# A fused hybrid decoder trunk: gated linear attention on 64x64 tiles of the array, differential scores on row halves

## The chip, the cores and the metric

The kernel runs on one core of one Trainium2 chip. The metric is the device time of one execution in microseconds (us). The engines of a core are TensorE (PE in the profile, its weight loads PEld), VectorE (DVE), ScalarE (ACT), GpSimd (POOL) and SyncE (SP), which here issues the weight transfers.

## The reference, cut to what matters

Two layers, 256 positions (two blocks of 128), width 4096, all in float32. Each layer normalises x, multiplies by a large `w_in`, feeds four token mixers, gates their output and multiplies by `w_out`. Two of the mixers are touched.

```python
# GLA, per head, chunks of C=64 positions, dk=64, dv=128 (8 heads, 4 chunks)
q_dec = q * dk**-0.5 * exp(b);  k_dec = k * exp(-b);  k_state = k * exp(b_last - b)
A       = where(causal, q_dec @ k_dec.T, 0)          # intra-chunk, within 64 positions
U       = k_state.T @ v                              # state of one chunk, 64 x 128
state   = exp(b_last) * state + U                    # state at the start of the next chunk
o       = A @ v + q_dec @ state_at_start             # intra + inter
# differential attention, per head: two maps (c = 0, 1) of 64 dimensions each
s[c]    = q[:, c] @ k[:, c].T                        # block 0: 128 keys, block 1: 256 keys
```

The state at the start of the first chunk is zero.

## The kernel before, in words

**The main products.** A layer is 31 chunks `j` of 512 output columns (23 of `w_in`, 8 of `w_out`), and a chunk is 16 groups `g` of two 128-row slices of the weights. For each group SP brings 512 KB of weights into `w_raw` (L220), ScalarE rounds them to `w_hi` (`hi`, L376), VectorE makes the rest `w_lo` (`lo`, L705), and TensorE runs `chunk_group` (L1140): 12 matmuls of 512 columns, six for each block of 128 positions. The three weight buffers have four slots each, so ScalarE and VectorE are at most four groups ahead of TensorE. At the end of a chunk ScalarE copies the two `main` banks out (`project`), in its own program after `hi` of groups 0 and 1 of the next chunk.

**The mixers** are cut into pieces, and every engine's program has the same loop over layer, chunk and group: after its share of group `g` of chunk `j` an engine runs the pieces that are hooked there. An order written out by hand, so: a piece stands at a group number, and semaphores hold it until its inputs are there. On TensorE every piece goes between the last matmul of one group and the first of the next.

**GLA** handles two heads per unit, one unit in each of chunks 4 to 7 (four units per layer, eight in all). The two heads' 64 dimensions lie on partitions 0 to 63 and 64 to 127. TensorE's pieces (`gla`, L1213): g 1 logits (contraction over 33 rows, L1221), g 3 sums, g 6 four transposes and U, g 8 the intra scores AT, g 11 the outputs. U is three matmuls of 256 columns, one for each chunk of 64 positions but the last; the other half of the 128 contraction rows in `g_ks` is zero, and of the 128x256 result the two diagonal blocks are used. AT is four matmuls of 128 columns against `g_q0` or `g_q1`, in which the other head's rows are zero. The output is eight matmuls with 64 output partitions (inter, two column halves of the array) and four with 128 (intra):

```python
for bank, off, t, c in ((4, 0, 0, 0), (4, 256, 0, 1), (5, 0, 1, 0)):                    # U, L1245
    ins = mm(M[bank][:, off:off + 256], g_ks[:, t, c, :], Y[:, t, vcol:vcol + 2 * P], off == 0, True)
...
            mm(M[1][r, b * P:(b + 1) * P], (g_q0, g_q1)[h][:, t * P + c * DK:t * P + (c + 1) * DK],
               g_S[:, 2 * t + c, :], b == 0, False)                                     # inter, L1263
```

Between them VectorE makes the states from U (g 10, six instructions on 64 partitions, L742 to L750) and copies AT (g 11, L754), POOL masks it (`mask_intra`, L292), and ScalarE copies the transposes (g 10, L414 to L416). At g 15 ScalarE squares the outputs (L419), VectorE sums them (L757), ScalarE makes the reciprocal root (L389, L391) and VectorE scales (L763). In chunk 7 TensorE also turns the keys of the sliding-window mixer at g 10 (L1391), which ScalarE copies at g 13 (L429). In chunk 6 `turn_rx` (L1209) stands at g 11, right behind the GLA outputs.

**Differential attention** handles two heads in each of chunks 16 to 19 (16 units in all). "turn" at g 0 and g 7, "scores" at g 1 and g 8 (L1320 to L1325): for each of the two maps a matmul of 128 and one of 256 columns, contracting over 128 rows of which 64 are zero in `d_q[c]`.

A float32 matmul that is not of the rounded kind stands in the profile as two records. Sixteen records of an inter step are its eight matmuls.

## Time and profile before

| | us |
|---|---|
| median of 3 runs | 2926.52 (2926.36 to 2926.75) |
| the profiled execution's own time | 2925.76 |
| its span, first to last instruction | 2924.0 |
| TensorE matmuls busy | 2913.5 (100%) |
| TensorE weight loads busy | 2403.2 (82%) |
| VectorE busy | 1585.6 (54%) |
| ScalarE busy | 1460.5 (50%) |
| GpSimd busy | 59.1 (2%) |
| DMA engines, mean busy share | 0.61, 187 GB/s |

A matmul's record in the profile has a modelled end and reaches into the next one, so what a matmul costs is read from the distance between starts. Idle time of an engine that is not the bottleneck costs nothing.

### The profile page before, as it was taken

The numbers are of one execution on the slowest core, as the hardware profiler recorded it, in microseconds if no ns is written. First come the engines' busy times: TensorE is split into PE (matmuls) and PEld (weight loads), VectorE is DVE, ScalarE is ACT, GpSimd is POOL, SyncE is SP. The second block draws the span as 40 slices with busy tenths as digits, with TensorE's granted clock in tenths as the row PEclk, the third lists the DMA queues.
The fourth block names the chain that finished last, engine by engine and source line by source line (L and its number), as shares of the span: only waits on it lengthen the run. The fifth ranks groups of instructions, "written<-read, shape, count | busy, mean of one in ns | idle before, by whom it ended". The sixth has DMA issues, their size and how long they took to land.

```text
span 2924.0 us, 34611 instructions
## 1 busy us (share of the span) xinstructions
PE 2913.5 (100%) x13381; PEld 2403.2 (82%) x13381; DVE 1585.6 (54%) x2098; ACT 1460.5 (50%) x2077; POOL 59.1 (2%) x106
## 2 busy tenths in 40 slices
PE   9999999999999999999999999999999999999999
PEld 7878888888888888888888888888888888888887
DVE  6445555555666455444554445555556664554444
ACT  6344445555566555444554444455555665553333
POOL 2000000000000000000000000000000000000000
PEclk9999999999999999999999999999999999999999
DMA  8655556666555666666666555565656565666664
GB/s 255 194 164 168 159 171 183 186 184 181 175 166 166 194 187 194 216 221 201 217 200 182 177 160 160 174 185 180 185 170 185 159 179 177 202 202 204 226 221 165
DMA packets 282965, 546.47 MB, mean 187 GB/s; under 512 B 17753, under 2 KB 22497, under 8 KB 282801
## 3 DMA queue, kind: packets, MB, share of 16 engines
q1 hardware_dynamic: 272560, 524.88, 58.5%
q0 software_dynamic: 5552, 17.26, 2.0%
q10 hardware_dynamic: 4688, 2.13, 0.3%
q8 instruction: 105, 1.72, 0.2%
q14 instruction: 60, 0.48, 0.0%
HBM read 535.81 MB, written 8.39 MB: 186 GB/s over the span
## 4 chain that ended last, share of the span: by engine, by line
PE 99%; ACT 0%; issue 0%; DMA 0%; DVE 0%; SPq 0%; ACTq 0%
PE main L1138 93%; PE mixer L1138 5%; PE mixer L1353 0%; PE mixer L1178 0%; PE mixer L1166 0%; PE mixer L1289 0%; PE mixer L1329 0%; DMA w_raw<-in_w_in 0%; PE mixer L1209 0%; PE mixer L1316 0%; PE mixer L1317 0%; PE mixer L1279 0%; ACT w_hi L376 0%; DVE w_lo L705 0%; PE mixer L1239 0%
## 5 line engine op out<-in xcount | busy, mean ns | idle before, releaser
L1138 PE MATMUL main<-w_hi,act 128*128 128x512 f32 x7936 | 2523.9, 394 | 1.8 <-ACT stage L386 0.9
L705 DVE TENSOR_TENSOR w_lo<-w_raw,w_hi 128x1024 fp32r<-128x1024 f32 x992 | 1205.7, 1224 | 1161.6 <-ACT w_hi L376 1155.1
L1138 PEld LDWEIGHTS main<-w_hi,act 128*128 128x128 f32 x7936 | 1490.9, 188 | 318.7 <-ACT act_T L386 2.8
L1138 PE MATMUL main<-w_lo,act 128*128 128x512 f32 x3968 | 1546.0, 390 | 0.0
L376 ACT ACTIVATE w_hi<-w_raw 128x1024 fp32r<-128x1024 f32 x992 | 1042.2, 1058 | 1001.6 <-PE main L1138 935.0
L1138 PEld LDWEIGHTS main<-w_lo,act 128*128 128x128 f32 x3968 | 746.4, 188 | 149.1
L386 ACT ACTIVATE stage<-main,rstd 128x512 f32<-128x512 f32 x40 | 27.4, 684 | 59.0 <-PE main L1138 58.4
L386 ACT ACTIVATE act_T<-main,rstd 128x512 f32<-128x512 f32 x28 | 19.1, 682 | 71.4 <-PE main L1138 71.4
L386 ACT ACTIVATE mix_Y<-main,rstd 128x512 f32<-128x512 f32 x24 | 16.4, 682 | 68.2 <-PE main L1138 68.2
L685 DVE SCALAR_TENSOR_TENSOR act<-act_T,par,act 128x256 fp32r<-128x256 f32 x96 | 42.0, 479 | 15.2 <-ACT act L358 15.1
L937 DVE TENSOR_TENSOR mix<-mix,main 128x512 f32<-128x512 f32 x32 | 22.0, 688 | 42.6 <-PE main L1138 42.6
L358 ACT ACTIVATE act<-act_T,par 128x256 fp32r<-128x256 f32 x96 | 43.0, 495 | 0.1
L1138 PE MATMUL mixer<-act_T,mix 128*128 128x128 f32 (+1 forms) x256 | 39.6, 288 | 0.0
L1138 PEld LDWEIGHTS mixer<-act_T,mix 128*128 128x128 f32 x256 | 36.0, 191 | 4.1
L499 ACT ACTIVATE mix<-mixer 128x128 f32<-128x128 f32 x32 | 8.5, 273 | 58.6 <-PE mixer L1138 58.6
L389 ACT ACTIVATE small<-small,cst 128x2 f32<-128x2 f32 (+2 forms) x50 | 14.8, 295 | 29.9 <-DVE small L873 29.2
L315 POOL DMA_DIRECT2D out<-mix x15 | 11.0, 731 | 915.8 <-DVEq L939 915.8
L1138 PE MATMUL mixer<-mix 128*128 128x256 f32 (+2 forms) x160 | 29.2, 321 | 0.0
L1138 PEld LDWEIGHTS mixer<-mix 128*128 128x128 f32 (+1 forms) x160 | 22.8, 190 | 5.6 <-issue 2.8
L296 POOL TENSOR_SCALAR_AFFINE_SELECT act_T<-act_T 128x512 f32<-128x512 f32 x8 | 12.4, 1551 | 693.5 <-DVE act_T L754 693.5
L491 ACT ACTIVATE mix<-mix,small 128x128 f32<-128x128 f32 x32 | 12.6, 395 | 25.6 <-DVE small L896 25.6
L838 DVE SCALAR_TENSOR_TENSOR mix<-mix_Y,par,mix 128x255 f32<-128x255 f32 (+2 forms) x48 | 23.2, 484 | 1.7
(234 smaller groups left out, 1052.4 us busy)
## 6 DMA issues: line engine op xcount, KB each, us to landing
w_raw<-in_w_in SPq DMA_DIRECT2D x736, 512.0 KB, 3.7
w_raw<-in_w_out SPq DMA_DIRECT2D x256, 512.0 KB, 3.7
out<-mix POOLq DMA_DIRECT2D x15, 512.0 KB, 3.5
mix<-in_x POOLq DMA_DIRECT2D x8, 512.0 KB, 6.0
mix<-out POOLq DMA_DIRECT2D x8, 512.0 KB, 6.1
mix_Y<-in_x SPq DMA_DIRECT2D x7, 512.0 KB, 7.2
act_T<-in_lru_w_r ACTq DMA_DIRECT2D x16, 64.0 KB, 1.8
act_T<-in_lru_w_i ACTq DMA_DIRECT2D x16, 64.0 KB, 2.0
```

The source lines that it names most:

```text
L296: pool.affine_select(out=AT, in_=AT, compare_op=ALU.is_ge, fill=0.0, base=0, pattern=[[0, 4], [1, P]], channel_multiplier=-1).then_inc(G[" ...
L315: pool.dma_start(out[0, :, i * NC:(i + 1) * NC].rearrange("(t p) n -> p t n", p=P), x_new).then_inc(x_stored, 16)
L358: ins = act.activation(A[:, k, 0, :], F[:, k * SEQ:(k + 1) * SEQ], ACT.Copy, scale=par[:, layer, base + k:base + k + 1])
L376: act.activation(w_hi[:, n % HI, :, :], w_raw[:, n % RAW, :, :], ACT.Copy).then_inc(w_hi_ready, 1)
L386: act.activation(dst[:, t, :], main[t][:, :], func, scale=rstd[:, t:t + 1]).then_inc(main_free, 1)
L389: act.activation(dst, src, ACT.Ln, scale=1.0 / n, bias=eps[:, :]).then_inc(ln, 1)
L491: act.activation(d_p[:, b:b + P], d_s[:, b:b + P], ACT.Exp, bias=d_sm[:, 20 + c:21 + c], accum_out=d_sm[:, 24 + c:25 + c])
L685: ins = dve.scalar_tensor_tensor(out=A[:, k, 1, :], in0=F[:, k * SEQ:(k + 1) * SEQ], scalar=par[:, layer, base + k:base + k + 1], in1=A[:, ...
L705: dve.tensor_tensor(w_lo[:, n % LO, :, :], w_raw[:, n % RAW, :, :], w_hi[:, n % HI, :, :].bitcast(F32), ALU.subtract).then_inc(w_lo_ready, 1)
L838: dve.scalar_tensor_tensor(out=l_xc[:, 3 - q:SEQ], in0=rx[:, i, 0:SEQ - 3 + q], scalar=p(q), in1=l_xc[:, 3 - q:SEQ], op0=ALU.mult, op1=ALU ...
L937: dve.tensor_tensor(x_new[:, t, :], x_old[:, t, :], main[t][:, :], ALU.add).then_inc(main_free, 1)
L1138: return pe.matmul(out_, lhsT, rhs, start=start, stop=stop, skip_group_check=True)
```

## The change

**Places of the array.** U, AT and the inter products now contract over 64 rows and give 64 output partitions: each is on one of four 64x64 tiles of the array (row half by the operands' partitions, column half by the output's). U is six matmuls of 128 columns, now at g 9, AT eight of 64 columns behind it in the same piece, the inter product six of 128 columns at g 13 (the first chunk's zero state is left out), the intra product four on the whole array as before. The row halves write to different banks: U's by chunk (M[4], M[5]), AT's and the outputs' by head (M[0] and M[2]; M[1] and M[3]). The differential scores contract over 64 rows with 128 output partitions, one map on each row half. Zero filling of `g_ks`, `g_q0`, `g_q1` and `d_q` goes; `g_AT`'s off-diagonal blocks are zeroed once per layer.

**Hooks.** ScalarE's copy of the transposes goes from g 10 to g 8, VectorE's states from g 10 to g 11, TensorE's AT from g 8 to g 9 and its outputs from g 11 to g 13; `turn_rx` of chunk 6 from g 11 to g 14 with its copy in g 2 of chunk 7; the turn of the keys in chunk 7 from g 10 to g 14 with its copy at g 15.

```diff
...
-g_ks = F[:, 4096:4608].rearrange("p (t c n) -> p t c n", t=T, c=2)
-g_q0, g_q1, g_kT = F[:, 4608:4864], F[:, 4864:5120], F[:, 5120:5376]
+g_ks = F[:, 4096:4352].rearrange("p (t n) -> p t n", t=T)
+g_qT, g_kT = F[:, 4608:4864], F[:, 4864:5120]
...
-g_AT = F[:, 5888:6400]
+g_AT = F[:, 5888:6400].rearrange("p (t h n) -> p t h n", t=T, h=2)
...
-d_q = (cut(1024, 256), cut(1280, 256))
+d_qT = cut(1024, 256)
...
     def mask_intra(layer, i):
...
-        AT = g_AT.rearrange("p (u i) -> p u i", u=4)
...
-        pool.affine_select(out=AT, in_=AT, compare_op=ALU.is_ge, fill=0.0, base=0,
-                           pattern=[[0, 4], [1, P]], channel_multiplier=-1).then_inc(G["ATmasked"], 1)
-        pool.wait_ge(G["ATmasked"], u * 2 + 1)
-        pool.memset(AT[0:DK, :, DK:P], 0.0).then_inc(G["ATmasked"], 1)
+        for c in range(2):
+            r = slice(c * DK, (c + 1) * DK)
+            AT = g_AT[r, :, :, c * DK:(c + 1) * DK].rearrange("p t h n -> p (t h) n")
+            pool.affine_select(out=AT, in_=AT, compare_op=ALU.is_ge, fill=0.0, base=0,
+                               pattern=[[0, 4], [1, DK]], channel_multiplier=-1).then_inc(G["ATmasked"], 1)
...
-        if g == 10:
+        if g == 8:
...
-            act.activation(g_q0[0:DK, :], M[3][0:DK, 0:256], ACT.Copy)
-            act.activation(g_q1[DK:P, :], M[3][DK:P, 0:256], ACT.Copy)
-            act.activation(g_kT, M[3][:, 256:512], ACT.Copy).then_inc(G["qkT"], 1)
+            act.activation(F[:, 4608:5120], M[3][:, :], ACT.Copy).then_inc(G["qkT"], 1)
         if g == 15:
...
-            act.activation(g_sq, M[1][:, :], ACT.Square).then_inc(G["sq"], 1)
+            for h in range(2):
+                ins = act.activation(g_sq[:, h * 256:(h + 1) * 256], M[1 + 2 * h][:, 0:256], ACT.Square)
+            ins.then_inc(G["sq"], 1)
...
-        if g == 13:
+        if g == 15:
...
         if s == "turned":
...
-            act.wait_ge(diff_zero, layer + 1)
-            act.activation(d_q[0][0:DK, :], M[0][0:DK, 0:256], ACT.Copy, scale=par[0:DK, layer, Q_DQ:Q_DQ + 1])
-            act.activation(d_q[1][DK:P, :], M[0][DK:P, 0:256], ACT.Copy, scale=par[DK:P, layer, Q_DQ:Q_DQ + 1])
+            act.activation(d_qT, M[0][:, 0:256], ACT.Copy, scale=par[:, layer, Q_DQ:Q_DQ + 1])
...
-                if j == J_RX[0] + 1 and g == 13:
+                if j == J_RX[0] + 2 and g == 2:
                     copy_rx(layer, 0, 0, 4)
...
-            for c in range(2):
-                r = slice(c * DK, (c + 1) * DK)
-                ins = dve.tensor_tensor(g_ks[r, :, c, :], gk[r, :, i * P:(i + 1) * P],
-                                        v3(g_es)[r, :, :], ALU.mult)
-            ins.then_inc(G["kst"], 1)
-        if g == 10:
+            dve.tensor_tensor(g_ks, k, v3(g_es), ALU.mult).then_inc(G["kst"], 1)
+        if g == 11:
...
-            for c, (bank, off) in enumerate(((4, 0), (4, 256), (5, 0))):
-                if c:
-                    dve.wait_ge(G["S"], u * 3 + c)
-                for h in range(2):
-                    r = slice(h * DK, (h + 1) * DK)
-                    src = M[bank][r, off + h * P:off + (h + 1) * P]
-                    if c == 0:
-                        ins = dve.tensor_copy(g_S[r, 1, :], src)
-                    else:
-                        ins = dve.scalar_tensor_tensor(out=g_S[r, c + 1, :], in0=g_S[r, c, :],
-                                                       scalar=g_dec[r, c:c + 1], in1=src,
-                                                       op0=ALU.mult, op1=ALU.add)
+            for k, (bank, off) in enumerate(((4, 0), (5, 0), (4, P))):
+                src = M[bank][:, off:off + P]
+                if k == 0:
+                    ins = dve.tensor_copy(g_S[:, 1, :], src)
+                else:
+                    dve.wait_ge(G["S"], u * 3 + k)
+                    ins = dve.scalar_tensor_tensor(out=g_S[:, k + 1, :], in0=g_S[:, k, :],
+                                                   scalar=g_dec[:, k:k + 1], in1=src,
+                                                   op0=ALU.mult, op1=ALU.add)
                 ins.then_inc(G["S"], 1)
-        if g == 11:
             dve.wait_ge(G["AT"], u + 1)
-            dve.tensor_copy(g_AT, M[0][:, :]).then_inc(G["ATcopied"], 1)
+            for h in range(2):
+                for c in range(2):
+                    r = slice(c * DK, (c + 1) * DK)
+                    ins = dve.tensor_copy(g_AT[r, :, h, c * DK:(c + 1) * DK],
+                                          M[2 * h][r, 0:P].rearrange("p (t n) -> p t n", t=T))
+            ins.then_inc(G["ATcopied"], 1)
         if g == 15:
...
             for t in range(T):
                 for h in range(2):
-                    b = (2 * t + h)
-                    ins = dve.tensor_scalar(Y[:, t, vcol + h * P:vcol + (h + 1) * P], M[1][:, b * P:(b + 1) * P],
+                    b = 2 * h + t
+                    ins = dve.tensor_scalar(Y[:, t, vcol + h * P:vcol + (h + 1) * P],
+                                            M[1 + 2 * h][:, t * P:(t + 1) * P],
...
-                    dve.memset(g_ks, 0.0)
-                    dve.memset(g_q0, 0.0)
-                    dve.memset(g_q1, 0.0)
-                    dve.memset(g_S[:, 0, :], 0.0).then_inc(gla_zero, 1)
+                    dve.memset(F[:, 5888:6400], 0.0).then_inc(gla_zero, 1)
...
                     if g == 15:
-                        dve.memset(d_q[0], 0.0)
-                        dve.memset(d_q[1], 0.0).then_inc(diff_zero, 1)
...
             ins.then_inc(G["turned"], 1)
+        if g == 9:
             pe.wait_ge(G["kst"], u + 1)
...
                 pe.wait_ge(rx_F, layer * 4 + 2)
-            for bank, off, t, c in ((4, 0, 0, 0), (4, 256, 0, 1), (5, 0, 1, 0)):
-                ins = mm(M[bank][:, off:off + 256], g_ks[:, t, c, :], Y[:, t, vcol:vcol + 2 * P], off == 0, True)
+            for t, c in ((0, 0), (0, 1), (1, 0)):
+                r = slice(c * DK, (c + 1) * DK)
+                for h in range(2):
+                    ins = mm(M[4 + c][h * DK:(h + 1) * DK, t * P:(t + 1) * P], g_ks[r, t, h * DK:(h + 1) * DK],
+                             Y[r, t, vcol + h * P:vcol + (h + 1) * P], t == 0, True)
             ins.then_inc(G["U"], 1)
-        if g == 8:
             pe.wait_ge(G["qkT"], u + 1)
-            for t in range(T):
+            pe.wait_ge(G["dec"], u + 1)
+            for t in range(T):
+                for c in range(2):
+                    tok = slice(t * P + c * DK, t * P + (c + 1) * DK)
+                    for h in range(2):
+                        r = slice(h * DK, (h + 1) * DK)
+                        ins = mm(M[2 * h][c * DK:(c + 1) * DK, t * DK:(t + 1) * DK], g_kT[r, tok], g_qT[r, tok],
+                                 t == 0, True)
+            ins.then_inc(G["AT"], 1)
+        if g == 13:
+            pe.wait_ge(G["S"], u * 3 + 3)
+            for k in (2, 1, 3):
+                t, c = divmod(k, 2)
+                tok = slice(t * P + c * DK, t * P + (c + 1) * DK)
                 for h in range(2):
-                    b = 2 * t + h
-                    ins = mm(M[0][:, b * P:(b + 1) * P], g_kT[:, t * P:(t + 1) * P],
-                             (g_q0, g_q1)[h][:, t * P:(t + 1) * P], b == 0, True)
-            ins.then_inc(G["AT"], 1)
-        if g == 11:
-            pe.wait_ge(G["S"], u * 3 + 3)
-            for c in range(2):
-                r = slice(c * DK, (c + 1) * DK)
-                for t in range(T):
-                    for h in range(2):
-                        b = 2 * t + h
-                        mm(M[1][r, b * P:(b + 1) * P], (g_q0, g_q1)[h][:, t * P + c * DK:t * P + (c + 1) * DK],
-                           g_S[:, 2 * t + c, :], b == 0, False)
+                    r = slice(h * DK, (h + 1) * DK)
+                    mm(M[1 + 2 * h][c * DK:(c + 1) * DK, t * P:(t + 1) * P], g_qT[r, tok], g_S[r, k, :], k < 3, False)
             pe.wait_ge(G["ATmasked"], u * 2 + 2)
             for t in range(T):
                 for h in range(2):
-                    b = 2 * t + h
-                    ins = mm(M[1][:, b * P:(b + 1) * P], g_AT[:, b * P:(b + 1) * P],
+                    ins = mm(M[1 + 2 * h][:, t * P:(t + 1) * P], g_AT[:, t, h, :],
...
             pe.wait_ge(DF["qkT"], u + 1)
             for c in range(2):
-                mm(M[1 + c][:, 0:P], d_q[c][:, 0:P], d_kT[:, 0:P], True, True)
-                ins = mm(M[1 + c][:, P:3 * P], d_q[c][:, P:2 * P], d_kT, False, True)
+                r = slice(c * DK, (c + 1) * DK)
+                mm(M[1 + c][:, 0:P], d_qT[r, 0:P], d_kT[r, 0:P], True, True)
+            for c in range(2):
+                r = slice(c * DK, (c + 1) * DK)
+                ins = mm(M[1 + c][:, P:3 * P], d_qT[r, P:2 * P], d_kT[r, :], False, True)
             ins.then_inc(DF["scores"], 1)
...
-                if j == J_RX[0] + 1 and g == 11:
+                if j == J_RX[0] + 1 and g == 14:
                     turn_rx(layer, 0, 0, 4)
...
                     turn_rx(layer, 1, (4, 10).index(g), 4)
-                if j == J_KEYS and g == 10:
+                if j == J_KEYS and g == 14:
                     pe.wait_ge(K["kn"], layer + 1)
...
```

TensorE, U and AT of the first GLA unit. Before, U stands behind the transposes of g 6 (`mixer<-mix_Y,act_T`) and AT (`mixer<-act_T`) two groups later. The rows around U:

```order
L1138 MATMUL main<-w_hi,act 128x512
L1238 MATMUL mixer<-ident,mix 128x128
L1239 MATMUL mixer<-ident,mix 128x128
L1238 MATMUL mixer<-ident,mix 128x128
L1239 MATMUL mixer<-ident,mix 128x128
L1138 MATMUL mixer<-mix_Y,act_T 128x256 x3
L1138 MATMUL main<-w_hi,act 128x512
```

Of the change, at g 9:

```order
L1129 MATMUL main<-w_lo,act 128x512
L1129 MATMUL main<-w_hi,act 128x512
L1129 MATMUL mixer<-mix_Y,act_T 64x128 x6
L1129 MATMUL mixer<-act_T 64x64 x8
L1129 MATMUL main<-w_hi,act 128x512
L1129 MATMUL main<-w_lo,act 128x512
```

U has moved back three groups and stands ahead of AT, between the same two main matmuls.

TensorE, the scores of the first differential head, before:

```order
L1138 MATMUL main<-w_hi,act 128x512
L1138 MATMUL mixer<-mix 128x128
L1138 MATMUL mixer<-mix 128x256
L1138 MATMUL mixer<-mix 128x128
L1138 MATMUL mixer<-mix 128x256
L1138 MATMUL main<-w_hi,act 128x512
```

Of the change:

```order
L1129 MATMUL main<-w_lo,act 128x512
L1129 MATMUL main<-w_hi,act 128x512
L1129 MATMUL mixer<-mix 128x128 x2
L1129 MATMUL mixer<-mix 128x256 x2
L1129 MATMUL main<-w_hi,act 128x512
```

The two maps now take turns; the number of matmuls and their columns are the same.

ScalarE, the end of chunk 7 and the start of chunk 8, before (L429 is the copy of the turned keys, L419 to L391 the norm of the GLA outputs, L376 `hi`, L386 the copy of a main bank):

```order
L376 ACTIVATE w_hi<-w_raw 128x1024 x3
L429 ACTIVATE act_T<-mixer,par 128x512
L376 ACTIVATE w_hi<-w_raw 128x1024 x2
L419 ACTIVATE mix<-mixer 128x512
L389 ACTIVATE act_T<-act_T,cst 128x4
L391 ACTIVATE act_T<-act_T 128x4
L376 ACTIVATE w_hi<-w_raw 128x1024
L386 ACTIVATE stage<-main,rstd 128x512
```

Of the change:

```order
L376 ACTIVATE w_hi<-w_raw 128x1024 x7
L418 ACTIVATE mix<-mixer 128x256 x2
L389 ACTIVATE act_T<-act_T,cst 128x4
L391 ACTIVATE act_T<-act_T 128x4
L429 ACTIVATE act_T<-mixer,par 128x512
L376 ACTIVATE w_hi<-w_raw 128x1024
L386 ACTIVATE stage<-main,rstd 128x512
```

The copy of the keys now stands behind the norm, right ahead of `hi` of chunk 8's first group.

## Rows read from the trace of the kernel before

**Rows 1.** The profile's page: busy time by engine, and the chain that ended last
```profile
PE 2913.5 (100%) x13381; PEld 2403.2 (82%) x13381; DVE 1585.6 (54%) x2098; ACT 1460.5 (50%) x2077; POOL 59.1 (2%) x106
...
PE main L1138 93%; PE mixer L1138 5%; PE mixer L1353 0%; PE mixer L1178 0%; PE mixer L1166 0%; PE mixer L1289 0%; PE mixer L1329 0%; DMA w_raw<-in_w_in 0%; PE mixer L1209 0%; PE mixer L1316 0%; PE mixer L1317 0%; PE mixer L1279 0%; ACT w_hi L376 0%; DVE w_lo L705 0%; PE mixer L1239 0%
```

**Rows 2.** The page's costliest groups: count | busy us, mean ns | idle before, releaser
```profile
L1138 PE MATMUL main<-w_hi,act 128*128 128x512 f32 x7936 | 2523.9, 394 | 1.8 <-ACT stage L386 0.9
L705 DVE TENSOR_TENSOR w_lo<-w_raw,w_hi 128x1024 fp32r<-128x1024 f32 x992 | 1205.7, 1224 | 1161.6 <-ACT w_hi L376 1155.1
...
L1138 PE MATMUL main<-w_lo,act 128*128 128x512 f32 x3968 | 1546.0, 390 | 0.0
L376 ACT ACTIVATE w_hi<-w_raw 128x1024 fp32r<-128x1024 f32 x992 | 1042.2, 1058 | 1001.6 <-PE main L1138 935.0
...
L296 POOL TENSOR_SCALAR_AFFINE_SELECT act_T<-act_T 128x512 f32<-128x512 f32 x8 | 12.4, 1551 | 693.5 <-DVE act_T L754 693.5
```

**Rows 3.** Timeline, TensorE, GLA unit of chunk 5: start us, us, engine, line, what
```profile
221.35 1.46 PE L1138 MATMUL mixer<-mix_Y,act_T 128*128 128x256 f32 x6
...
222.89 0.40 PE L1138 MATMUL main<-w_lo,act 128*128 128x512 f32 x1
...
228.14 1.05 PE L1138 MATMUL mixer<-act_T 128*128 128x128 f32 x8
...
229.26 0.40 PE L1138 MATMUL main<-w_lo,act 128*128 128x512 f32 x1
...
236.98 0.39 PE L1138 MATMUL main<-w_hi,act 128*128 128x512 f32 x1
237.30 1.58 PE L1138 MATMUL mixer<-act_T 128*64 128x128 f32 x16
238.81 1.16 PE L1138 MATMUL mixer<-mix_Y,act_T 128*128 128x128 f32 x8
...
240.04 0.39 PE L1138 MATMUL main<-w_lo,act 128*128 128x512 f32 x1
```

**Rows 4.** Timeline, TensorE, differential scores of the first head in chunk 16
```profile
786.25 1.47 PE L1138 MATMUL mixer<-mix 128*128 128x128 f32 x8
...
787.79 0.39 PE L1138 MATMUL main<-w_lo,act 128*128 128x512 f32 x1
```

**Rows 5.** Timeline, TensorE, logits of chunk 4, contracting over 33 rows
```profile
204.84 0.39 PE L1138 MATMUL main<-w_hi,act 128*128 128x512 f32 x1
205.15 0.71 PE L1138 MATMUL mixer<-mix 33*128 33x128 f32 x4
...
206.13 0.39 PE L1138 MATMUL main<-w_lo,act 128*128 128x512 f32 x1
```

**Rows 6.** Two windows in the inter step, mixer matmuls: us, busy (records), granted clock, DMA
```profile
237.55:237.65 0.10, 0.10 (x3) 1.00 0.01 0
238.05:238.15 0.10, 0.10 (x7) 1.00 1.04 61
```

**Rows 7.** Timeline, weight loads of the inter step, [idle before]
```profile
237.30 1.34 PEld L1138 LDWEIGHTS mixer<-act_T 128*64 128x64 f32 x16 [0.35 <-issue]
```

**Rows 8.** Timeline, ScalarE and VectorE around the GLA norm and the state step, chunk 5
```profile
224.03 1.45 DVE L748 SCALAR_TENSOR_TENSOR act_T<-act_T,mixer 64x128 f32<-64x128 f32 x4
...
240.01 0.60 ACT L419 ACTIVATE mix<-mixer 128x512 f32<-128x512 f32 x1 [1.48 <-PE mixer L1138]
240.64 0.69 DVE L757 TENSOR_REDUCE act_T<-mix 128x4 f32<-128x512 f32 x1 [0.85 <-ACT mix L419]
241.36 0.30 ACT L389 ACTIVATE act_T<-act_T,cst 128x4 f32<-128x4 f32 x1 [0.75 <-DVE act_T L757]
241.69 0.20 ACT L391 ACTIVATE act_T<-act_T 128x4 f32<-128x4 f32 x1
```

**Rows 9.** Timeline, the turn of the keys in chunk 7 and ScalarE's copy of it
```profile
388.64 0.60 PE L1391 MATMUL mixer<-ident,mix 128*128 128x128 f32 x4
...
389.28 0.69 ACT L429 ACTIVATE act_T<-mixer,par 128x512 f32<-128x512 f32 x1 [2.04 <-PE mixer L1391]
```

More of the change, by code:

```diff
@@ L162, in hybrid_trunk @@
         gate_mult, gate_T, gate_F = sem("gate_mult"), sem("gate_turned"), sem("gate_ready")
-        gla_zero, diff_zero = sem("gla_zero"), sem("diff_zero")
+        gla_zero = sem("gla_zero")
         rx_out, rx_T, rx_F = sem("rx_out"), sem("rx_turned"), sem("rx_copied")
```

## The prediction

> **What bounds the kernel now.** I read the page first: TensorE is busy for the whole span, every other engine for about half of it, and the chain that ended last is 99% TensorE: 93% the main products, 5% the mixers' matmuls [rows 1]. Then the costliest groups: the main matmuls idle 1.8 us in all [rows 2], so no wait ends late anywhere. A microsecond of TensorE's queue is a microsecond of the kernel, and other engines count only where they would make TensorE wait. The granted clock is 1.00, TensorE's 2.4 GHz level [rows 6]; nothing in the change lets the engine idle, so it stays. Last, the timeline for the price of each piece. Between pieces a main matmul starts every 0.227 us: (236.98 - 229.26) / 34 [rows 3]. A piece costs the time from its first start to the second main start behind it, less one 0.227 (the first main record starts early and waits); with a change of array shape ahead of it I count from the last main start before, less two.
>
> **Prices before** [rows 3, 4]. U: 222.89 - 221.35 - 0.23 = 1.31. AT: 229.26 - 228.14 - 0.23 = 0.89, for eight records, so 0.112 for a record of 128 columns. Outputs: 240.04 - 236.98 - 0.45 = 2.61, of which the eight intra records take 0.90 and the inter step 1.71. Scores: 787.79 - 786.25 - 0.23 = 1.31 (eight records, two of 128 and two of 256 columns for each map).
>
> **Changing the shape of the array has a price.** The logits contract over 33 rows and so use a row part of the array: four records that would take 0.45 cost 206.13 - 204.84 - 0.45 = 0.84 [rows 5]. Going in and coming back costs 0.39. In the inter step the weights are 64 columns, not 128: their load is idle 0.35 us before the first [rows 7], and a first load of half the columns should take about half a record less, 0.05 (estimate), so I take 0.34 for a pair of changes into tiles with 64 columns. The inter products themselves then take 1.71 - 0.34 = 1.37.
>
> **Column tiles work side by side, and the engine looks ahead only a little.** Sixteen records in 1.37 us is 0.086 each, under 0.11. The windows show why: early in the step 3 records overlap a window of 0.1 us, later 7 do [rows 6]. The first eight records are on the left columns, the next eight on the right. Eight in a row take 8 x 0.11 = 0.88, so the right half ended 0.49 later: it started 0.49 after the left, when four and a half records of it had gone. I read this as a look-ahead of about three records past the running one, each tile with its own stream, its own weight load included. The change puts only two records in a row on a tile before it goes to the next, so this look-ahead is enough to keep all tiles fed.
>
> **The change part by part.** (Row halves are nowhere seen side by side before; I assume of them what the column halves show. Bounds in the rivals.)
>
> 1. *U and AT, one piece in 64x64 tiles at g 9.* U: six matmuls are 12 records of 128 columns; the order left, right on the upper rows, left, right on the lower, left, right on the upper gives the busiest tile four: 0.44. AT: 16 records of 64 columns, four for each tile, 0.055 each (half of 0.11, estimate): 0.22. With one hold-up of half a record by the look-ahead: 0.715. A pair of shape changes: 0.34. Sum 1.055 against 1.31 + 0.89 = 2.20: **-1.15** a unit. Bounds: with every record alone it would be 12 x 0.11 + 16 x 0.055 + 0.34 = 2.54, that is +0.34; below, nothing under 0.66 + 0.34.
> 2. *Inter product at g 13.* 12 records; the order is upper left, lower left, upper right, lower right, and the last two again. The right tiles have four records and start half a record late: 0.44 + 0.055 = 0.495 against 1.37: **-0.875**. The shape changes and the intra product are as before. One chunk's product less is in this (bound: 12 x 0.11 = 1.32, so -0.05 with every record alone).
> 3. *Scores.* Each map on its own row half, half of 1.31 each: 0.655; plus a pair of changes with 128 weight columns, 0.39: 1.045 against 1.31: **-0.27**. Alone: +0.39. This is the part in which a new price eats most of the gain.
>    The Trainium skill (TensorE: Matmul & The Clock Gate, Part 3) gives 3.07 times, not 4, for four row tiles of 512 columns; no run here shows row tiles yet. By that loss two row halves would take 1.31 / 1.53 = 0.86, the scores -0.06, and the sum would be some 3 us less of a gain.
> 4. *ScalarE's and VectorE's pieces.* Fewer and wider instructions; the mask on POOL shrinks from 1.55 us [rows 2] to two halves on a quarter of the elements each. All hidden as long as weights stay ahead, so what each moved wait holds up counts. At g 11 VectorE now waits for U and AT of g 9, with `lo` of group 12 behind it: three state steps and four small copies, at most the old 1.45 [rows 8] plus four of 0.3, and 1.22 for `lo` itself [rows 2] make 3.9 us after the piece; TensorE needs it after two groups, 5.4 us. Hidden, 1.5 us to spare. ScalarE's copy at g 8 waits for the transposes of g 6, with `hi` 9 and `lo` 9 behind: about 0.7 + 0.7 + 1.06 + 1.22 = 3.7 against 5.4. Hidden. The outputs move from g 11 to g 13 and the norm at g 15 is held longer; in chunks 4 to 6 `lo` of the next chunk is ready about 0.8 us early.
> 5. *The end of chunk 7.* There the copy of the keys stands behind the norm. Count from the last main start of g 13. The squares start 240.01 - 236.98 = 3.03 later before [rows 8], now 3.03 - 0.875 = 2.15; two squares of about 0.4, the sum 0.69, 0.30 and 0.20 with 0.03 between them end at 4.2. The turn of the keys starts after the outputs (1.73) and 13 main matmuls (2.95), at 4.7, and the copy 0.64 after that [rows 9], so it ends at 6.0. `hi` 1.06 and `lo` 1.22 [rows 2] follow: 8.2. TensorE comes to chunk 8 at 25 x 0.227 + 1.73 + 0.44 = 7.85. A new wait of **0.4 us**, once a layer: +0.8. It was hidden before because copy and norm were two groups and more earlier.
> 6. `turn_rx`, zero fills: nothing on TensorE beyond the same transposes in another place.
>
> Sum: 8 x (-1.15 - 0.875) = -16.2; 16 x (-0.27) = -4.3; +0.8. **-19.7 us**. The profiled execution's own time is 2925.76; it becomes 2906.1. The median shown is 0.76 above that execution, so I predict 2906.8.
>
> **The rivals.**
>
> *Issue sets the pace (chance 0.12).* The 0.49 of the inter step is also 8 x 0.061: if after the array has emptied TensorE issues one record in 0.061 us, whatever the tile, the rows look the same. Then U and AT take 28 x 0.061 + 0.34 = 2.05 (-0.15), the inter step 0.84 (-0.53), the scores 0.78 + 0.39 (-0.14): -5.5 - 2.3 + 0.8 = -7.0, 2919.5. Against it: the queue has many main matmuls of 0.227 in which to fill.
> The Trainium skill (same page, Part 1) gives 62 ns of the sequencer's firmware for a matmul when the hardware does not decode it, which is this pace; it would bind in AT above all.
>
> *Weight loads of the two row halves go one after the other (0.12).* A load takes as long as a record of 128 columns for 128 weight columns, half of that for 64. The scores then need eight loads in a row and the last record: 1.10 + 0.39 (+0.18); U and AT 0.94 + 0.34 (-0.93), inter 0.60 (-0.77): -13.6 + 2.9 + 0.8 = -9.9, 2916.6.
>
> *Row halves take turns altogether (0.07).* Column tiles still pair. U and AT 1.21 + 0.34 (-0.65), inter 0.93 (-0.44), scores 1.30 + 0.39 (+0.38): -8.7 + 6.1 + 0.8 = -1.8, 2924.7, within what can be told from no change.
>
> *The other side: each turn from one row half to the other empties the array (0.05).* A change of shape costs half a pair, 0.17 to 0.2, and if a change of row half does too, the 9 turns of U and AT, 5 of the inter step and 3 of the scores add 8 x 14 x 0.17 + 16 x 3 x 0.2 = 28.6 to the case before: +26.8, 2953. It makes the kernel slower as soon as a turn costs 1.8 / 160 = 0.011 us. For it: no row before shows a turn of row halves. Against it: the turn from left to right columns empties nothing [rows 6].
>
> The change does what it says: the order of the instructions shows the smaller matmuls. The last 0.02 is for waits on VectorE or ScalarE that I have not seen.
>
> **How the numbers follow.** The forecast has 0.62 and its own range is 2904 to 2910 (look-ahead a little longer or shorter, no wait or a double one in chunk 8, the skill's loss on row tiles). The range reaches up over the two rivals next to it, to 2921: 0.86 of the cases, of which some lie outside my sizes. Two tenths of a per cent are 5.9 us, about what a measurement of this kernel tells from no change. Faster by more: the forecast, the serial loads and most of the issue case, 0.82. Within: row halves in turns and the rest of the issue case, 0.12. Slower: 0.06.
>
> **What would show it.** In the profile after: U and AT as one piece that costs TensorE about 1.05 us between main matmuls, outputs about 1.73, scores about 1.05; many mixer records overlapping in one window of the 64x64 piece; one wait of some 0.4 us of a main matmul for `lo` at the start of chunk 8, none elsewhere; main matmuls still 0.227 apart. Wrong would be: records in the 64x64 piece 0.06 apart (issue), scores above 1.31 (row halves in turns or loads in a row), or main matmuls waiting for `lo` in every chunk end.

## The result and the profile after

| | before | after |
|---|---|---|
| median of the runs, us | 2926.44 (2925.84 to 2926.75, 4 runs) | 2905.09 (2904.76 to 2905.81, 4 runs) |
| the profiled execution's own time | 2925.76 | 2904.84 |
| span of the profiled execution | 2924.0 | 2903.1 |

The ratio is 0.9929, with a 95% interval of 0.9916 to 0.9941: 21.35 us between the medians, 20.92 between the two profiled executions. The forecast was 2906.8, in a range of 2903.5 to 2921.0. So the sum of -19.7 fell short by 1.2 us, or 6%; the other 0.5 us between forecast and median is that this median lies only 0.25 above its own profiled execution, where before's lay 0.76 in the three runs that the forecast had.

The page after, its line of busy times and the group of the main products, which answer to [rows 1, 2]:

```profile
PE 2892.3 (100%) x13461; PEld 2373.4 (82%) x13461; DVE 1576.7 (54%) x2080; ACT 1445.9 (50%) x2053; POOL 66.2 (2%) x106
...
L1129 PE MATMUL main<-w_hi,act 128*128 128x512 f32 x7936 | 2522.3, 394 | 2.0 <-ACT stage L386 0.9
```

TensorE is still busy from end to end, and the main products still wait for next to nothing. TensorE has 80 records more than before and is busy 21.2 us less (2892.3 against 2913.5): records are smaller and lie beside each other. The granted clock is 1.00 as before.

**U and AT.** The timeline of TensorE after, in the GLA unit of chunk 5 (start us, length us, engine, line, what), against the first four rows of [rows 3]:

```profile
229.44 0.39 PE L1129 MATMUL main<-w_hi,act 128*128 128x512 f32 x1
229.75 0.55 PE L1129 MATMUL mixer<-mix_Y,act_T 64*64 64x128 f32 x10
230.04 0.27 PE L1129 MATMUL mixer<-act_T 64*64 64x64 f32 x2
...
230.14 0.27 PE L1129 MATMUL mixer<-mix_Y,act_T 64*64 64x128 f32 x1
230.15 0.49 PE L1129 MATMUL mixer<-act_T 64*64 64x64 f32 x13
230.57 0.50 PE L1129 MATMUL main<-w_hi,act 128*128 128x512 f32 x1
230.90 0.39 PE L1129 MATMUL main<-w_lo,act 128*128 128x512 f32 x1
```

The piece costs 230.90 - 229.44 - 0.45 = 1.01 us, where U and AT were 1.31 and 0.89. Its 28 records (12 of U, 16 of AT) start between 229.75 and the first main record at 230.57: 0.82 / 28 = 0.029 us each. AT's first records (230.04) start while U's last are still to come (230.14): a tile that has done its part of U goes on alone.

**Outputs.** The same view, a little later, against the last four rows of [rows 3]:

```profile
241.35 0.39 PE L1129 MATMUL main<-w_hi,act 128*128 128x512 f32 x1
241.67 0.67 PE L1129 MATMUL mixer<-act_T 64*64 64x128 f32 x12
242.27 1.16 PE L1129 MATMUL mixer<-mix_Y,act_T 128*128 128x128 f32 x8
...
243.50 0.39 PE L1129 MATMUL main<-w_lo,act 128*128 128x512 f32 x1
```

243.50 - 241.35 - 0.45 = 1.70 us against 2.61. The intra records are what they were; the inter step went from 1.51 (237.30 to 238.81 [rows 3]) to 0.60 between the first starts.

**Scores.** The same view in chunk 16, against [rows 4]:

```profile
777.97 0.39 PE L1129 MATMUL main<-w_hi,act 128*128 128x512 f32 x1
778.29 0.93 PE L1129 MATMUL mixer<-mix 64*128 64x128 f32 x8
...
779.48 0.39 PE L1129 MATMUL main<-w_lo,act 128*128 128x512 f32 x1
```

779.48 - 777.97 - 0.45 = 1.06 us against 1.31.

**Overlap.** Two windows of 0.1 us, one in each kind of 64x64 piece, mixer matmuls alone (us, busy and how many records, granted clock, DMA), against [rows 6]:

```profile
229.85:229.95 0.10, 0.10 (x8) 1.00 1.11 430
241.85:241.95 0.10, 0.10 (x8) 1.00 0.22 82
```

Eight records reach into each window, where the column halves alone showed 3 and 7. A record's end is modelled, so the count tells how densely records start; the pace of 0.029 us a record above says the same.

**The new wait.** TensorE's waits in the whole span of after, without the two of its start (waited for: us in total, times, longest):

```profile
PE main L1129 <- ACT stage L386: 0.9, 2, 0.4
PE main L1129 <- DVE act L692: 0.6, 1, 0.6
PE main L1129 <- DVE w_lo L703: 0.5, 2, 0.2
```

The last line is new: two waits for `w_lo`, one a layer. The timeline shows the first, at the start of chunk 8:

```profile
396.89 0.39 PE L1129 MATMUL main<-w_hi,act 128*128 128x512 f32 x1
397.52 0.50 PE L1129 MATMUL main<-w_hi,act 128*128 128x512 f32 x1 [0.24 <-DVE w_lo L703]
397.86 0.40 PE L1129 MATMUL main<-w_lo,act 128*128 128x512 f32 x1
398.10 0.62 PE L1129 MATMUL main<-w_hi,act 128*128 128x512 f32 x2
398.56 0.39 PE L1129 MATMUL main<-w_lo,act 128*128 128x512 f32 x1
```

The second start is 0.63 behind the first instead of 0.227, so 0.40 late; with the stretched step behind it (0.34) the loss is 397.86 - 396.89 - 0.45 = 0.52. In return another loss is gone. This is the same place in the trace of before:

```profile
406.47 0.91 PE L1138 MATMUL main<-w_hi,act 128*128 128x512 f32 x2
407.21 0.39 PE L1138 MATMUL main<-w_lo,act 128*128 128x512 f32 x1
```

There the second bank began late: 407.21 - 406.47 - 0.45 = 0.29, against 398.56 - 398.10 - 0.45 = 0.01 after. Net 0.52 + 0.01 - 0.29 = +0.24 a layer. The second of these losses stands in no wait of TensorE's matmuls. The weight loads' own list (PEld) has it: before, in chunk 8, the load for the second bank waits 0.44 us for ScalarE's copy (L386).

The account, from the starts on record, which have one digit more than the view prints: U and AT 1.30 + 0.90 to 1.02, the outputs 2.60 to 1.69, so 8 x (-1.18 - 0.91) = -16.7; each scores piece 0.27 less, so 16 x (-0.27) = -4.3; chunk 8 in both layers 2 x 0.24 = +0.5. That makes -20.5 of the measured -20.92. Of the other 0.4, 0.23 is a stop ahead of chunk 28 of the second layer that the trace of before has and that of after has not (2790.24 - 2789.56 - 0.45); no cause of it is on record. The start of the kernel varies by more than that: in the profiled executions of all these kernels the first twelve main matmuls took from 4.3 to 5.7 us (before 4.9, after 5.1).

### The profile page after: what moved, and what is told of

It reads as the page before. It is cut to its first block, busy times and chain, and to the rows that moved or that the text cites. A ratio compares the mean times of both kernels' runs of the same rounds, so it can differ in the third digit from the quotient of the medians.

```text
span 2903.1 us, 34721 instructions
## 1 busy us (share of the span) xinstructions
PE 2892.3 (100%) x13461; PEld 2373.4 (82%) x13461; DVE 1576.7 (54%) x2080; ACT 1445.9 (50%) x2053; POOL 66.2 (2%) x106
## 4 chain that ended last, share of the span: by engine, by line
PE 99%; ACT 0%; issue 0%; DVE 0%; DMA 0%; SPq 0%; ACTq 0%
PE main L1129 93%; PE mixer L1129 4%; PE mixer L1351 0%; PE mixer L1169 0%; PE mixer L1157 0%; PE mixer L1284 0%; PE mixer L1327 0%; DMA w_raw<-in_w_in 0%; PE mixer L1312 0%; PE mixer L1200 0%; PE mixer L1274 0%; PE mixer L1311 0%; ACT w_hi L376 0%; DVE w_lo L703 0%; PE mixer L1230 0%
## 5 line engine op out<-in xcount | busy, mean ns | idle before, releaser
L376 ACT ACTIVATE w_hi<-w_raw 128x1024 fp32r<-128x1024 f32 x992 | 1041.4, 1058 | 966.8 <-PE main L1129 909.4
L386 ACT ACTIVATE act_T<-main,rstd 128x512 f32<-128x512 f32 x28 | 19.1, 682 | 68.2 <-PE main L1129 68.2
L386 ACT ACTIVATE stage<-main,rstd 128x512 f32<-128x512 f32 x40 | 27.3, 684 | 38.3 <-PE main L1129 37.7
L386 ACT ACTIVATE mix_Y<-main,rstd 128x512 f32<-128x512 f32 x24 | 16.4, 682 | 59.2 <-PE main L1129 59.2
L298 POOL TENSOR_SCALAR_AFFINE_SELECT act_T<-act_T 64x256 f32<-64x256 f32 x16 | 21.9, 1370 | 681.3 <-DVE act_T L747 680.8
```

The lines of the kernel that those rows point to most:

```text
L298: pool.affine_select(out=AT, in_=AT, compare_op=ALU.is_ge, fill=0.0, base=0, pattern=[[0, 4], [1, DK]], channel_multiplier=-1).then_inc(G[ ...
L376: act.activation(w_hi[:, n % HI, :, :], w_raw[:, n % RAW, :, :], ACT.Copy).then_inc(w_hi_ready, 1)
L386: act.activation(dst[:, t, :], main[t][:, :], func, scale=rstd[:, t:t + 1]).then_inc(main_free, 1)
```

## The experiments

Theory T, from the prediction: tiles stream and load side by side, row halves as well as column halves; each tile keeps about three records behind the running one; a change of the array's shape has a price of its own. Rivals: issue at 0.06 us a record sets the pace; row halves do not pair, or load in a row. Later a fourth, on what the look-ahead is. Where no span is named, times are medians, with the kernel before run on the same chip. The 95% intervals are 5 to 10 us wide, so the small steps rest on the timelines.

### The two halves of the change, alone

Scores on row halves in the kernel before, with one copy of the queries instead of two zero-filled ones:

```diff
...
                     for c in range(2):
-                        mm(M[1 + c][:, 0:P], d_q[c][:, 0:P], d_kT[:, 0:P], True, True)
-                        ins = mm(M[1 + c][:, P:3 * P], d_q[c][:, P:2 * P], d_kT, False, True)
+                        r = slice(c * DK, (c + 1) * DK)
+                        mm(M[1 + c][:, 0:P], d_qT[r, 0:P], d_kT[r, 0:P], True, True)
+                    for c in range(2):
+                        r = slice(c * DK, (c + 1) * DK)
+                        ins = mm(M[1 + c][:, P:3 * P], d_qT[r, P:2 * P], d_kT[r, :], False, True)
```

> The kernel before with the differential scores alone on row halves; GLA as before. If row halves stream and load side by side: each of the 16 scores pieces falls from 1.31 to about 1.04 us between main matmuls (0.655 of stream, 0.39 for a pair of shape changes), 16 x 0.27 = 4.3 us less, about 2922. If the two row halves took turns: 16 x 0.38 = 6 us more, about 2932. If only their weight loads did: 16 x 0.18 = 3 us more.

The kernel after with this part taken back:

```diff
...
                     for c in range(2):
-                        r = slice(c * DK, (c + 1) * DK)
-                        mm(M[1 + c][:, 0:P], d_qT[r, 0:P], d_kT[r, 0:P], True, True)
-                    for c in range(2):
-                        r = slice(c * DK, (c + 1) * DK)
-                        ins = mm(M[1 + c][:, P:3 * P], d_qT[r, P:2 * P], d_kT[r, :], False, True)
+                        mm(M[1 + c][:, 0:P], d_q[c][:, 0:P], d_kT[:, 0:P], True, True)
+                        ins = mm(M[1 + c][:, P:3 * P], d_q[c][:, P:2 * P], d_kT, False, True)
```

> The changed kernel with the scores back on the whole array against zero-filled queries (and the zero fill back), GLA on 64x64 tiles as changed. If the terms are additive: 4.3 us more than the changed kernel, about 2909.4, and 17 us less than the kernel before: 8 x (1.15 + 0.9) less 1. If GLA's gain leant on the scores' (a shared wait on VectorE or ScalarE), it would be off by a microsecond or more.

The scores alone: 2921.19 (2920.76 to 2922.35, 10 runs) against 2926.26, ratio 0.9983 (0.9974 to 0.9993), -5.1 us. The GLA part alone: 2910.31 (2908.83 to 2910.75), ratio 0.9944 (0.9929 to 0.9959), 5.2 us above the whole change, and its GLA pieces stay at 1.02 and 1.70. In the first one's timeline the scores of chunk 16 have their last main start before at 785.96 and the second behind at 787.47: 1.51 - 0.45 = 1.06, with no GLA change near them. -0.27 x 16 = -4.3 explains most of the -5.1; the two parts add (5.07 + 15.95 = 21.0 of 21.35). Loads in a row (1.49) and row halves in turns (1.69) are out.

### AT apart from U

AT waits one group longer, so that the engine changes its shape twice instead of once.

```diff
                     ins.then_inc(G["U"], 1)
+                if g == 10:
                     pe.wait_ge(G["qkT"], u + 1)
```

> The changed kernel with AT one group later than U (g 10, not g 9), so two pieces in 64x64 tiles in place of one. If the price is the change of shape: one more pair of changes a unit, 8 x 0.34 = 2.7 us more, 2907.8, perhaps 0.05 more a unit since AT no longer fills U's idle tiles (3.1). If changing the shape cost nothing and the 0.39 of the logits came from the 33 rows: no difference.

Measured 2908.89 (2908.16 to 2909.69), ratio 0.994 (0.9925 to 0.9955); that is 3.8 above after; the span is 2906.4, 3.3 above after's. TensorE's timeline, U and then AT of chunk 5:

```profile
229.41 0.39 PE L1129 MATMUL main<-w_hi,act 128*128 128x512 f32 x1
229.73 0.65 PE L1129 MATMUL mixer<-mix_Y,act_T 64*64 64x128 f32 x12
...
230.65 0.40 PE L1129 MATMUL main<-w_lo,act 128*128 128x512 f32 x1
...
232.94 0.39 PE L1129 MATMUL main<-w_hi,act 128*128 128x512 f32 x1
233.26 0.46 PE L1129 MATMUL mixer<-act_T 64*64 64x64 f32 x16
...
233.99 0.39 PE L1129 MATMUL main<-w_lo,act 128*128 128x512 f32 x1
```

0.79 and 0.60 make 1.39 against 1.01: a second pair of changes costs 0.38 us, in which lies whatever is lost because AT no longer starts beside U's last records. 8 x 0.38 = 3.0 of the 3.3. The sixteen records of AT end within 0.60 with that pair in it; one each 0.06 us would need 1.0 for issue alone.

### What the look-ahead is

First the inter step of after, by heads: three matmuls on tiles of the upper rows, then three on the lower.

```diff
...
-                    for k in (2, 1, 3):
-                        t, c = divmod(k, 2)
-                        tok = slice(t * P + c * DK, t * P + (c + 1) * DK)
-                        for h in range(2):
+                    for h in range(2):
+                        for k in (2, 1, 3):
+                            t, c = divmod(k, 2)
+                            tok = slice(t * P + c * DK, t * P + (c + 1) * DK)
...
```

> The changed kernel with the six inter products ordered by head: upper left, upper right twice, lower left, lower right twice, instead of turning between heads. Same matmuls, same tiles. If the engine looks only some three records past the running one: the lower tiles start later, the step grows from 0.49 to about 0.65 us, 8 x 0.16 = 1.3 us more (2906.4). If it looked over the whole queue, or if issue at a fixed pace set the time: within 0.1 us a unit of the changed kernel.

Measured 2905.32 (2905.01 to 2905.81), ratio 0.9928 (0.9911 to 0.9944): no difference from after. The outputs stand between main starts at 241.62 and 243.78: 2.16 - 0.45 = 1.71, against 1.70. This was a miss of mine: I had expected the lower tiles to start late, as if the engine saw a fixed stretch of its queue. They don't, so that stretch is not what limits. What fits this and the 0.49 of before is that a record is held up only when its own tile, or the tile of one ahead of it in the queue, has about three waiting: here no tile gets more than four in a row. That reading says what the kernel before would do if its eight left records came in runs of four:

```diff
...
-                    for c in range(2):
-                        r = slice(c * DK, (c + 1) * DK)
-                        for t in range(T):
+                    for t in range(T):
+                        for c in range(2):
+                            r = slice(c * DK, (c + 1) * DK)
...
```

> The kernel before with its eight inter products in another order: four records on the left columns, four on the right, and again, in place of eight and eight. Only the order changes. If each tile can hold about three records behind the running one, whatever stands on other tiles: both halves start together, the inter step falls from 1.37 to 0.88 us of stream, 8 x 0.49 = 3.9 us less, 2922.5. If the engine looks over a fixed stretch of the whole queue (six loads and matmuls not yet issued): the right half starts a record late each time, stream about 1.2, 1.3 us less. If issue at 0.061 us a record set the 0.49: stream 0.98 + 0.05, 2.7 us less.

Measured 2922.52 (2921.93 to 2923.1, 10 runs) against 2926.14, ratio 0.9988 (0.9978 to 0.9997). Its inter step on TensorE:

```profile
236.92 0.39 PE L1138 MATMUL main<-w_hi,act 128*128 128x512 f32 x1
237.24 1.15 PE L1138 MATMUL mixer<-act_T 128*64 128x128 f32 x16
238.32 1.16 PE L1138 MATMUL mixer<-mix_Y,act_T 128*128 128x128 f32 x8
...
239.55 0.39 PE L1138 MATMUL main<-w_lo,act 128*128 128x512 f32 x1
```

From the first inter start to the first intra start it is 1.08 us instead of 1.51 [rows 3], with the same sixteen records in another order: -0.43 x 8 = -3.4, and -3.6 was measured between the medians. The expectation had -0.49 for it, a fixed stretch of the queue -0.16 and issue at a fixed pace -0.34. So 0.43 of the 0.91 us that the change gains on the outputs could be had without 64x64 tiles, by order alone. (The change also leaves out the first chunk's product. No run has that part alone. By the prices it saves nothing: that product lies on the left columns, and the busiest tile has four records with it or without.)

Last, the scores of after with each map's two matmuls together, runs of four for each row half:

```diff
                         mm(M[1 + c][:, 0:P], d_qT[r, 0:P], d_kT[r, 0:P], True, True)
-                    for c in range(2):
-                        r = slice(c * DK, (c + 1) * DK)
                         ins = mm(M[1 + c][:, P:3 * P], d_qT[r, P:2 * P], d_kT[r, :], False, True)
```

> The changed kernel with each map's 128-column and 256-column scores behind each other (the order of before, four records in a row on a row half) instead of the maps taking turns. With about three records held behind the running one for each tile: no difference (piece 1.06 us). With a look-ahead over a fixed stretch of the whole queue: the second map starts a record late, 0.11 us a piece, 16 x 0.11 = 1.8 us more.

Measured 2904.78 (2904.6 to 2904.89), ratio 0.9926 (0.9911 to 0.9941): no difference from after, as a run of four should. The profiled execution even started 0.5 us faster than after's. The interleaving of the scores in the change is not needed.

### The wait at chunk 8

The turn of the keys and its copy two groups and one group earlier:

```diff
-                if g == 15:
+                if g == 14:
                     act.wait_ge(K["turned"], layer + 1)
...
-                        if j == J_KEYS and g == 14:
+                        if j == J_KEYS and g == 12:
                             pe.wait_ge(K["kn"], layer + 1)
+                            pe.wait_ge(G["ATcopied"], layer * 4 + 4)
```

> The changed kernel with the turn of the keys at g 12 (not 14) and ScalarE's copy at g 14 (not 15), ahead of the norm. If the 0.54 us that the keys' piece costs above its four transposes is ScalarE's late hi of chunk 8: the wait of a main matmul for lo at the start of chunk 8 goes, 2 x 0.54 = 1.1 us less, about 2904.0. If that time belonged to the outputs' two-group delay itself (norm at g 15), the wait stays and the time is the changed kernel's.

Measured 2905.03 (2904.46 to 2905.8), ratio 0.9928 (0.9911 to 0.9944): no difference from after. The wait for `w_lo` is gone from the list of TensorE's waits, here without the two of its start:

```profile
PE main L1129 <- DVE act L692: 1.3, 1, 1.3
PE main L1129 <- ACT stage L386: 0.9, 2, 0.4
```

But ScalarE's timeline at the start of chunk 8 shows what lay under it:

```profile
395.95 0.69 ACT L386 ACTIVATE stage<-main,rstd 128x512 f32<-128x512 f32 x1 [1.27 <-PE main L1129]
395.96 0.42 ACTq L456 DMA_DIRECT2D act_T<-in_lru_w_r  x1
396.42 0.45 ACTq L457 DMA_DIRECT2D act_T<-in_lru_w_i  x1
396.97 1.06 ACT L376 ACTIVATE w_hi<-w_raw 128x1024 fp32r<-128x1024 f32 x1 [0.33 <-issue]
397.94 0.67 ACT L386 ACTIVATE stage<-main,rstd 128x512 f32<-128x512 f32 x1
```

And TensorE's at the same time:

```profile
398.18 0.97 PE L1129 MATMUL main<-w_hi,act 128*128 128x512 f32 x2
398.99 0.39 PE L1129 MATMUL main<-w_lo,act 128*128 128x512 f32 x1
```

The copy of the second bank ends at 398.61, and the second of the two main matmuls at 398.18 can't start before: 398.99 - 398.18 - 0.45 = 0.36 late. The copy is late because `hi` ahead of it stands behind two DMA issues of 0.42 and 0.45 us on ScalarE's queue. A wait that a list names can be the cover of another: 0.52 went and 0.36 came, and the 0.16 a layer that is left is too little for the medians to show.

### The DMA issues out of the way

So in the kernel after ScalarE issues these two loads two groups later:

```diff
-                if g == 0:
+                if g == 2:
                     if u:
```

> The changed kernel with ScalarE's two weight transfers of the recurrent mixer issued at g 2 of chunks 8 to 15, not at g 0 between the copies of the two main banks. If their issue (0.36 and 0.45 us on ScalarE) makes the copy of the second bank late: the first group of each of these chunks, now 0.23 us (chunk 8: 0.13) over its twelve matmuls, comes down to 2.72, 14 x 0.23 + 2 x 0.13 = 3.5 us less, about 2901.6; the wait of 0.4 at the start of chunk 8 stays. If the 0.23 had another cause (the bank's own turnaround): no difference.

Measured 2902.93 (2900.9 to 2903.91), ratio 0.992 (0.9903 to 0.9936). TensorE's timeline at the start of chunk 9 in after:

```profile
446.23 0.82 PE L1129 MATMUL main<-w_hi,act 128*128 128x512 f32 x2
446.89 0.40 PE L1129 MATMUL main<-w_lo,act 128*128 128x512 f32 x1
```

The same place in this kernel:

```profile
446.28 0.62 PE L1129 MATMUL main<-w_hi,act 128*128 128x512 f32 x2
446.73 0.39 PE L1129 MATMUL main<-w_lo,act 128*128 128x512 f32 x1
```

0.66 becomes 0.45, 0.21 less, and over the twelve matmuls of the chunk's first group 0.23. The same stands at the start of each of the chunks 9 to 15 in both layers: 14 x 0.23 = 3.2. The spans differ by 2.5, since the start of this profiled execution was 0.7 us slower than that of after; the medians by 2.2. The list of waits of TensorE's matmuls has nothing of it, but the distance of the starts has, and so has the list of the weight loads' waits (PEld). In after it holds these fourteen for the copy of a bank, and here it holds none of them (waited for: us in total, times, longest):

```profile
PEld main L1129 <- ACT act_T L386: 2.8, 8, 0.4
PEld main L1129 <- ACT mix_Y L386: 2.1, 6, 0.4
```

### The logits on all rows, and the best version

The logits contract over 33 rows and pay the change of shape for it [rows 5]. Here both operands are filled with zeros up to 128 rows, on top of the earlier keys; the mask is one instruction again.

```diff
...
+                pool.memset(MIX[:, 2688:2944], 0.0)
+                pool.memset(MIX[:, 3072:3584], 0.0).then_inc(rank_zero, 1)
...
-                        ins = mm(M[0][:, t * P:(t + 1) * P], g_aT[:, t * P:(t + 1) * P],
-                                 g_wup[:, i * P:(i + 1) * P], t == 0, True)
+                        ins = mm(M[0][:, t * P:(t + 1) * P], MIX[:, 2688 + t * P:2688 + (t + 1) * P],
+                                 MIX[:, 3072 + i * P:3072 + (i + 1) * P], t == 0, True)
...
```

> The keys' turn early as in the run beside it, and two edits more: the GLA logits contract over 128 rows, of which all but 33 are zero in both operands, so that they stay in the whole array's shape; the mask is one instruction over all 128 partitions (the off-diagonal blocks are zero or cut by it). If the 0.39 of the logits is the change of shape and nothing of the 33 rows: 8 x 0.39 = 3.1 us less on top of 1.1, about 2900.9. If a matmul's rows cost something, less of it. The mask changes no time, since POOL has groups to spare; its busy time falls from 8 x 2.74 to 8 x 1.55 us.

Measured 2902.39 (2901.15 to 2903.02), ratio 0.9918 (0.9903 to 0.9932). Its logits on TensorE, against [rows 5]:

```profile
205.18 0.40 PE L1131 MATMUL main<-w_hi,act 128*128 128x512 f32 x1
205.42 0.61 PE L1131 MATMUL mixer<-mix 128*128 128x128 f32 x4
...
206.10 0.39 PE L1131 MATMUL main<-w_lo,act 128*128 128x512 f32 x1
```

0.47 instead of 0.84, for the same four records with four times the rows. It is the change of shape that costs, not the number of rows: 0.37 us a pair, times 8 is 3.0 us, where the median is 2.6 under that of the kernel with the keys alone. Its profiled execution started 0.3 us slower than that one's.

Finally all of it together: this kernel with the two DMA issues at g 2.

> All that gained, together: the changed kernel with the keys' turn early, logits in the whole array's shape, one mask instruction, and the two transfers at g 2. With the transfers out of the way the early keys' gain is no longer taken by the wait for the second bank in chunk 8 (0.38 there): 14 x 0.23 + 2 x 0.38 = 4.0 us under the kernel without the transfers' move, about 2898.4. If the keys' gain is lost to something else, 0.8 more than that.

Measured 2897.31 (2897.12 to 2897.65), ratio 0.9901 (0.9887 to 0.9916): 28.8 us under before and 7.8 under after, the fastest here. About 0.7 of the difference to after is the start of its profiled execution; the rest is in the pieces above. The start of chunk 8 in its timeline, where the starts are now at their distance of 0.45:

```profile
397.58 0.62 PE L1131 MATMUL main<-w_hi,act 128*128 128x512 f32 x2
398.03 0.39 PE L1131 MATMUL main<-w_lo,act 128*128 128x512 f32 x1
```

The 0.52 that after lost here is gone, and so is the 0.36 that had kept the earlier keys from showing a gain alone.

## Why the prediction was right

- **TensorE's queue is the kernel.** Right: what its pieces lost is what the time lost, 20.5 of 20.92 us.
- **U and AT as one piece, 1.055.** Measured 1.01 to 1.02. The share for a hold-up by the look-ahead (0.055) was too much: without it the prediction's own terms give 0.66 + 0.34 = 1.00.
- **Outputs 1.73.** Measured 1.70, for the same reason: 0.035 too much, 8 times. Both together are 0.6 of the 1.2 us that were missing, chunk 8 is 0.3 and the stop ahead of chunk 28 is 0.2.
- **Scores 1.045.** Measured 1.06, and alone in the kernel before 1.06 as well. The assumption that row halves behave as column halves, which no row before showed, held; it was assumed and not derived, and the range was made wide enough for two ways in which it could fail. The Trainium skill (TensorE: Matmul & The Clock Gate, Part 3) gives 3.07 times for four row tiles; by that loss, as an estimate, the scores would have taken 1.25, and here half the stream (0.66) and a pair of changes (0.39) make the whole.
- **The shape change, 0.39 and 0.34.** Held: 0.38 where AT was set apart (0.34 was the price there), 0.37 where the logits went to all rows. The trace agrees with the Trainium skill (TensorEngine Tiling (Array Packing), Key Properties), by which a change of tiling mode drains the array and a change of tile does not.
- **The wait at chunk 8, 0.4.** Its place, its size (0.40) and its number were right, its price of +0.8 was not. The wait also stretched the step behind it, so it cost 0.52, and it was counted on top, while the late second bank of before (0.29) vanished beneath it. Net +0.24 a layer, +0.5 in all: two errors of opposite sign, the largest single miss of the sum after the look-ahead's share.
- **Other engines hidden.** Right in effect. But the step had the mask on POOL shrink, and it grew. The group after, against the last row of [rows 2]:

```profile
L298 POOL TENSOR_SCALAR_AFFINE_SELECT act_T<-act_T 64x256 f32<-64x256 f32 x16 | 21.9, 1370 | 681.3 <-DVE act_T L747 680.8
```

Two instructions of 1.37 us take the place of one of 1.55 and a zero fill of 0.30. It costs nothing, since POOL idles 681 us there, and one mask over everything measured 1.68. The prediction scaled the mask with its elements. But every one of these masks ran beside VectorE's `lo`: in chunk 5 the first from 232.69 to 234.14 with `lo` from 232.65 to 233.88, and it ended 0.26 after it. The same kind of instruction at the kernel's start (L276, 128x256 elements, no VectorE work beside it) took 0.39. So much of the 1.37 looks like time in which POOL stands still for VectorE; no run sets the two apart.
- **Issue as the pace (chance 0.12).** Refuted: 0.029 us a record in U and AT. No run here shows the 62 ns of the Trainium skill (TensorE: Matmul & The Clock Gate, Part 1) as a bound.
- **Row halves in a row, in turns, or emptying the array (0.12, 0.07, 0.05).** Refuted: the scores cost 1.06 where these would have made 1.49, 1.69 and more.
- **The look-ahead.** It gave the right numbers for the change, in whose orders no tile gets more than two records in a row, but as I first used it (a fixed stretch of the queue, in the expectation of the inter step by heads) it was wrong. The two orders of the inter step before, 1.51 and 1.08, and the two inter orders of the change, 1.70 and 1.71, are what fixed it.

What stays open: the number of about three waiting records, which is worked out from the one run of eight (runs of five to seven on one tile weren't tried); how a tile's three waiting records are counted where records are longer than 128 columns, and what holds a few other chunk starts up. How the tiles of both operands would fare in quarters of the array wasn't tried.

## What to carry to other kernels

Matmuls that fill half of the array's rows or columns, or multiply zeros, can lie side by side: give each tile its share in runs of at most four records (eight held the other half up here, five to seven weren't tried), and put everything of one shape into one piece, since every other piece paid 0.38 us here to go in and out (and for a product too small to pair, fill the rows with zeros instead). Price a piece by the distance of the starts around it, not by the length of its records. Before a wait is priced or removed, look for what would end just behind it on the same engine: here a wait that cost 0.52 us covered one of 0.36, and removing it alone gave nothing that the medians could show. Read the waits of the weight loads beside those of the matmuls: the losses of 0.2 us at the chunk starts stood only there.

## What was not expected of the hardware

- A run of eight records on one column half delays the other half, one of four does not: 1.51 against 1.08 us for the same sixteen records.
- Four records over 33 rows cost more than four over 128, with the changes of shape around them: 0.84 against 0.47 us.
- A mask on POOL beside VectorE's `lo` takes 1.37 us for 64x256 elements and 1.55 to 1.68 for 128x512; one of 128x256 with VectorE idle took 0.39. And `lo` is slower beside it: in after the sixteen of 992 that start while a mask runs take 1.42 us, where the median is 1.22; before, none starts there and none takes over 1.23.
- A DMA issue on ScalarE's queue takes 0.33 to 0.46 us. At the start of a chunk two of them hold up the `hi` behind them, and moving them by two groups is worth 2 to 3 us (2.2 between the medians, 3.2 by the starts).
